# Three 256-column products into the same 256 columns, in place of a 512-column product, a 256-column one and a fold

## What is computed

```python
def glu_out(y, h):                      # end of the S5 mixer
    z = jax.nn.gelu(y...); a, g = jnp.split(z @ w_glu, 2, axis=-1)
    return a * jax.nn.sigmoid(g)

def sq_relu_mlp(h, w1, w2):             # w1: 2048 x 8192, w2: 8192 x 2048
    return jnp.square(jax.nn.relu(h @ w1)) @ w2

def swiglu(h, w_gate, w_up, w_down):    # D_FF = 5632
    return (jax.nn.silu(h @ w_gate) * (h @ w_up)) @ w_down

# first_block
x_lat = x_lat + gt1[:, None] * rmsnorm(y_lat, norm_mix_post[layer])
h_lat = modulate(rmsnorm(x_lat, norm_mlp_pre[layer]), sh2[:, None], sc2[:, None])
x_lat = x_lat + gt2[:, None] * rmsnorm(sq_relu_mlp(h_lat, ...), norm_mlp_post[layer])

# second_block
for layer in range(2):
    h = rms_norm(x, mix_norm_g[layer])
    if layer == 0:
        z = h @ ab_w_in[0]              # 2048 x 4096: a, gate, u, v, 1024 each
        y_conv = conv_module(z[..., :2048], ...)      # a * sigmoid(gate), 31 taps in time, layer norm, silu
        y_sgu = spatial_gating(z[..., 2048:], ...)    # gelu, layer norm of v, mixed over tokens, times u
        x = x + jnp.concatenate([y_conv, y_sgu], axis=-1) @ ab_w_out[0]
    else:
        x = x + fourier_mix(h) @ fnet_w_out[0] + fnet_b_out[0]
    h = rms_norm(x, ffn_norm_g[layer])
    x = x + swiglu(h, w_gate[layer], w_up[layer], w_down[layer])
return rms_norm(x, final_norm_g)
```

## Time and profile before

| | us |
|---|---|
| time, median of 3 (lowest, highest) | 3479.0 (3478.8, 3480.57) |
| time of the profiled execution | 3470.21 |
| span in its profile | 3468.3 |
| TensorE busy | 3227.5 (93%) |
| VectorE busy | 2201.4 (63%) |
| ScalarE busy | 1389.7 (40%) |
| GpSimd busy | 480.2 (14%) |
| granted clock of TensorE, mean | 0.96 |
| weights and all else read | 637.28 MB, 185 GB/s over the span |

### The profile page before, as it was taken

How to read it: one execution, slowest core, us unless ns; L and a number is a source line. 1 busy time by engine, 2 the same in 40 slices (tenths; PEclk the granted TensorE clock), 3 DMA queues, 4 the chain that set the end, 5 groups by cost and what they waited for, 6 DMA issues and landing times.

```text
span 3468.3 us, 51580 instructions
## 1 busy us (share of the span) xinstructions
PE 3227.5 (93%) x21009; PEld 2726.8 (79%) x21009; DVE 2201.4 (63%) x1891; ACT 1389.7 (40%) x1433; POOL 480.2 (14%) x352
## 2 busy tenths in 40 slices
PE   5788899799999999798599999999999999999998
PEld 3445578588888888676488888888878888888887
DVE  7668754555655555679757656665674765566565
ACT  4446643433333333332234434433333443443332
POOL 2979700000000000069000000000000000000000
PEclk7889999899999999998799999999999999999999
DMA  9998975355555555344145555555544555555552
GB/s 297 300 301 255 272 243 183 101 170 193 176 196 185 190 185 189 102 157 151 49 146 184 192 185 181 184 201 182 194 152 134 183 183 196 178 194 194 189 186 85
DMA packets 351027, 643.17 MB, mean 185 GB/s; under 512 B 21599, under 2 KB 50359, under 8 KB 350519
## 3 DMA queue, kind: packets, MB, share of 16 engines
q1 hardware_dynamic: 309952, 561.42, 49.7%
q10 hardware_dynamic: 40951, 79.98, 6.8%
HBM read 637.28 MB, written 4.06 MB: 185 GB/s over the span
## 4 chain that ended last, share of the span: by engine, by line
PE 82%; DVE 6%; DMA 3%; issue 3%; POOL 2%; ACT 2%; SPq 1%; DVEq 1%; ACTq 0%; POOLq 0%
PE acc L455 50%; PE acc L456 26%; DMA raw<-in_w_mod_dram 2%; PE acc L1274 1%; DVE z L1060 1%; DVE w_lo L849 1%; POOL cpow L1927 1%; PE acc L1366 1%; POOL ptmp L1927 1%; ACT u L1528 1%; PE acc L1349 1%; DMA tw<-r_scratch 1%; PE acc L475 0%; DMA r_scratch<-rw 0%; PE acc L553 0%
## 5 line engine op out<-in xcount | busy, mean ns | idle before, releaser
L849 DVE TENSOR_TENSOR w_lo<-raw,w_hi 128x2048 fp32r<-128x2048 f32 x484 | 1109.3, 2300 | 962.9 <-ACT w_hi L672 961.4
L455 PE MATMUL acc<-xin,w_hi 128*128 128x512 f32 x3968 | 1417.4, 400 | 44.0 <-DVE w_lo L849 24.1
L672 ACT ACTIVATE w_hi<-raw 128x2048 fp32r<-128x2048 f32 x484 | 924.7, 1917 | 1231.9 <-PE acc L456 1231.8
L455 PE MATMUL acc<-hid,w_hi 128*128 128x512 f32 x3840 | 1332.7, 391 | 0.0
L456 PE MATMUL acc<-xin,w_lo 128*128 128x256 f32 x3968 | 1122.5, 283 | 0.0
L456 PE MATMUL acc<-hid,w_lo 128*128 128x256 f32 x3840 | 1075.3, 280 | 0.0
L455 PEld LDWEIGHTS acc<-xin,w_hi 128*128 128x128 f32 x3968 | 752.1, 190 | 232.6 <-DVE w_lo L849 25.4
L455 PEld LDWEIGHTS acc<-hid,w_hi 128*128 128x128 f32 x3840 | 718.2, 187 | 157.9
L456 PEld LDWEIGHTS acc<-xin,w_lo 128*128 128x128 f32 x3968 | 755.4, 190 | 0.0
L456 PEld LDWEIGHTS acc<-hid,w_lo 128*128 128x128 f32 x3840 | 725.8, 189 | 0.1
L855 DVE TENSOR_REDUCE tmp<-acc 128x1024 f32<-128x2048 f32 x116 | 264.9, 2283 | 21.9 <-PE acc L456 21.9
(11 more groups left out here) (265 smaller groups left out, 2088.5 us busy)
## 6 DMA issues: line engine op xcount, KB each, us to landing
raw<-in_ffn_w_gate_dram SPq DMA_DIRECT2D x88, 1024.0 KB, 5.2
raw<-in_ffn_w_up_dram SPq DMA_DIRECT2D x88, 1024.0 KB, 5.2
raw<-in_ffn_w_down_dram SPq DMA_DIRECT2D x88, 1024.0 KB, 5.1
raw<-in_w_mod_dram ACTq DMA_DIRECT2D x76, 1024.0 KB, 8.9
raw<-in_w_mlp_in_dram SPq DMA_DIRECT2D x64, 1024.0 KB, 5.2
raw<-in_w_mlp_out_dram SPq DMA_DIRECT2D x64, 1024.0 KB, 5.1
raw<-in_s_w_glu_dram SPq DMA_DIRECT2D x32, 1024.0 KB, 5.4
raw<-in_ab_w_in_dram SPq DMA_DIRECT2D x32, 1024.0 KB, 5.3
```

What stands on the lines that cost most here:

```text
L455: pe.matmul(bank, w_hi[:, slot, w], operand[:, kt, :], start=(kt == 0), stop=False)
L672: act.activation(w_hi[:, slot, :], raw[:, slot, :, :].rearrange("p k n -> p (k n)"), ACT.Copy).then_inc(hi_ready, 1)
L849: dve.tensor_tensor(w_lo[:, slot, :], raw[:, slot, :, :].rearrange("p k n -> p (k n)"), w_hi[:, slot, :].bitcast(F32), SUB).then_inc(lo_re ...
```

## The change

In `block_` the tile becomes three matmuls of 256 columns: `w_hi` times the high columns, `w_hi` times the low columns and `w_lo` times the high columns, all accumulated in columns 0 to 255 of the bank. These columns of four banks have a name now, `sums[half]`, and nothing is left to fold. `fold` is a plain copy and stands in three places (the GLU's first half and two blocks of AB_IN); elsewhere the consumer reads the banks: ScalarE's sigmoid, gelu and a new relu, VectorE's products, and `fold_into`, which adds the sums to `y` or `xr`. The FFN adds its down blocks to `xr` directly, so the additions to `y`, the zeroing of `y` and the additions of `y` to `xr` are gone. In `gate_up` the second product with rstd is gone: rstd is multiplied to the gate twice, before and after silu. `folded` counts the release of the banks by whichever engine reads them, and takes over from several semaphores. ScalarE's reads of banks stand in its own program before the split that they once followed.

```diff
+        sums = [acc[:, 4 * h:4 * h + 4, 0:TOK] for h in range(2)]
...
@@ SyncE
-            sp.wait_ge(x_new, 4 * NCK)
+            sp.wait_ge(x_rs, 3)
             sp.dma_start(dft[:, :], a["c_dft"]).then_inc(dft_in, 16)
...
@@ TensorE, block_
-                            bank, kt = ps[4 * half + n], UK * k + q
-                            pe.matmul(bank, w_hi[:, slot, w], operand[:, kt, :], start=(kt == 0), stop=False)
-                            ins = pe.matmul(bank[:, 0:TOK], w_lo[:, slot, w], operand[:, kt, 0:TOK],
-                                            start=False, stop=(kt == UK * units - 1))
+                            o, kt = ps[4 * half + n][:, 0:TOK], UK * k + q
+                            pe.matmul(o, w_hi[:, slot, w], operand[:, kt, 0:TOK], start=(kt == 0), stop=False)
+                            pe.matmul(o, w_hi[:, slot, w], operand[:, kt, TOK:2 * TOK], start=False, stop=False)
+                            ins = pe.matmul(o, w_lo[:, slot, w], operand[:, kt, 0:TOK], start=False, stop=(kt == UK * units - 1))
...
@@ ScalarE, GLU
-                    split(g, slots=(2, 3))
-                act.wait_ge(folded, 2 * i + 2)
-                act.activation(tmp[:, 1], tmp[:, 1], ACT.Sigmoid).then_inc(gate_act, 1)
+                    split(g, slots=(2,))
+                    if g == 2 * i + 2:
+                        act.wait_ge(pe_unit, 4 * g)
+                        act.wait_ge(folded, 2 * i + 1)
+                        act.wait_ge(y_added, i + 1)
+                        act.activation(tmp[:, 1], sums[1], ACT.Sigmoid).then_inc(folded, 1)
+                    split(g, slots=(3,))
...
@@ ScalarE, MLP
                         split(8 * q + (2 * i + (G + 1 + j)))
-                        hidden(4 * q + (2 * i + j), 2 * i + j, j, hid)
+                        act.wait_ge(pe_unit, 32 * q + (8 * i + (MLP[0] + 4 * j + 4)))
+                        act.wait_ge(hid_ready, 4 * q + (2 * i + (j + 1)))
+                        act.activation(tmp[:, j], sums[j], ACT.Relu).then_inc(relu_done, 1)
+                        hidden(8 * q + (2 * i + (MLP[1] + j)), 2 * i + j, j, hid)
...
@@ ScalarE, AB_IN
+            for j in range(8):
+                split(G + 1 + j)
+                if j in (0, 2):
+                    continue
+                place, func = {1: (8, ACT.Sigmoid), 3: (12, ACT.Sigmoid)}.get(j, (4 * j, ACT.Gelu))
+                act.wait_ge(pe_unit, AB_IN[0] + 4 * j + 4)
+                act.wait_ge(folded, AB_IN[1] + j)
+                act.activation(z[:, place:place + 4, :], sums[j % 2], func).then_inc(folded, 1)
...
@@ VectorE
-            def fold(units_done, half, dst, done=None):
+            def fold(units_done, half, dst):
 
                 dve.wait_ge(pe_unit, units_done)
-                dve.tensor_reduce(dst, acc[:, 4 * half:4 * half + 4, :].rearrange("p a (t b) -> p a b t", t=2),
-                                  AX.X, ADD).then_inc(folded, 1)
+                dve.tensor_copy(dst, sums[half]).then_inc(folded, 1)
+
+            def fold_into(units_done, blk, half, dst):
+
+                dve.wait_ge(pe_unit, units_done)
+                dve.wait_ge(folded, blk)
+                dve.tensor_tensor(dst, dst, sums[half], ADD).then_inc(folded, 1)
...
@@ VectorE, gate_up of the FFN
                     split(grp + 1)
-                    dve.wait_ge(y_added, added)
                     dve.wait_ge(hid_ready, n + 1)
-                    fold(4 * grp + 4, 0, tmp[:, 0])
-                    dve.wait_ge(folded, blk + 1)
+                    dve.wait_ge(pe_unit, 4 * grp + 4)
+                    dve.wait_ge(folded, blk)
+                    dve.tensor_tensor(tmp[:, 0], sums[0], rstd, MUL).then_inc(folded, 1)
+                    split(grp + 2, (0,))
+                    dve.wait_ge(gate_act, gate + 1)
                     dve.tensor_tensor(tmp[:, 0], tmp[:, 0], rstd, MUL).then_inc(scaled, 1)
-                    split(grp + 2)
-                    fold(4 * grp + 8, 1, tmp[:, 1])
-                    dve.wait_ge(folded, blk + 2)
-                    dve.tensor_tensor(tmp[:, 1], tmp[:, 1], rstd, MUL).then_inc(scaled, 1)
-                    dve.wait_ge(gate_act, gate + 1)
-                    dve.wait_ge(scaled, nth + 2)
-                    dve.tensor_tensor(tmp[:, 1], tmp[:, 1], tmp[:, 0], MUL).then_inc(h_ready, 1)
+                    split(grp + 2, (1, 2, 3))
+                    dve.wait_ge(pe_unit, 4 * grp + 8)
+                    dve.wait_ge(scaled, gate + 1)
+                    dve.tensor_tensor(tmp[:, 1], sums[1], tmp[:, 0], MUL).then_inc(folded, 1)
                     hidden(n, c, 1, xin)
...
@@ VectorE, last part of the FFN
-                    add_to_y(4 * g2 + REST * (c + 1), b2 + c, c % 2, c, y1 + c, h1 + REST + 1)
-                    dve.wait_ge(y_added, y1 + c + 1)
-                    dve.tensor_tensor(xr[:, chunk(c), :], xr[:, chunk(c), :], y[:, chunk(c), :], ADD).then_inc(x_new, 1)
+                    fold_into(4 * g2 + REST * (c + 1), b2 + c, c % 2, xr[:, chunk(c), :])
...
@@ VectorE, AB_IN
             for j in range(8):
-                place = (0, 8, 4, 12, 16, 20, 24, 28)[j]
                 split(G + 1 + j)
-                fold(AB_IN[0] + 4 * j + 4, j % 2, z[:, place:place + 4, :])
+                if j in (0, 2):
+                    dve.wait_ge(folded, AB_IN[1] + j)
+                    fold(AB_IN[0] + 4 * j + 4, 0, z[:, 4 * (j // 2):4 * (j // 2) + 4, :])
...
@@ GpSimd
-            for n in (2, 4):
-                pool.wait_ge(x_rs, n + 1)
-                pool.memset(yflat, 0.0).then_inc(y_zero, 1)
```

More of the change, by code:

```diff
@@ L683, in seam @@
                     for c in range(NCK):
-                        act.wait_ge(y_added, (Y_MLP, Y_FFN0)[s.n] - NCK + c + 1)
+                        act.wait_ge(*((y_added, c + 2) if s.n == 0 else (folded, s.block - NCK + c + 1)))
                         act.activation(s.sq[:, CH * c:CH * (c + 1), :], y[:, CH * c:CH * (c + 1), :], ACT.Square).then_inc(y_sq, 1)
@@ L713, in join_raw, with hidden @@
                 act.activation(rs[:, 1, :], rs[:, 1, :], ACT.Sqrt).then_inc(x_root, 1)
-            def hidden(n, chunk, half, dst):
-                act.wait_ge(h_ready, n + 1)
+            def hidden(blk, chunk, half, dst):
+                act.wait_ge(folded, blk + 1)
                 act.activation(dst[:, ds(CH * chunk, CH) if not isinstance(chunk, int) else slice(CH * chunk, CH * (chunk + 1)), 0:TOK],
@@ L779, in GEMM_ACT @@
             G = AB_IN[0] // 4
-            for half in range(2):
-                split(G + 1 + 2 * half)
-                split(G + 2 + 2 * half)
-                act.wait_ge(folded, AB_IN[1] + 2 * half + 2)
-                gate = z[:, 8 + 4 * half:12 + 4 * half, :]
-                act.activation(gate, gate, ACT.Sigmoid).then_inc(gate_sig, 1)
-            with act.Fori(0, 2) as i:
-                split(i + (G + 5))
-            act.wait_ge(folded, AB_IN[1] + 6)
-            act.activation(z[:, 16:24, :], z[:, 16:24, :], ACT.Gelu).then_inc(u_gelu, 1)
-            with act.Fori(0, 2) as i:
-                split(i + (G + 7))
-            act.wait_ge(folded, AB_IN[1] + 8)
-            act.activation(z[:, 24:32, :], z[:, 24:32, :], ACT.Gelu).then_inc(v_gelu, 1)
+            for j in range(8):
[6 more added lines that the diff above has]
+                act.activation(z[:, place:place + 4, :], sums[j % 2], func).then_inc(folded, 1)
             act.wait_ge(ws_tr, 1)
@@ L1019, in GEMM_DVE @@
                 split(2 * i + 2)
-                fold(8 * i + 8, 1, tmp[:, 1])
-                dve.wait_ge(gate_act, i + 1)
+                dve.wait_ge(folded, 2 * i + 2)
                 dve.tensor_tensor(y[:, chunk(i), :], tmp[:, 0], tmp[:, 1], MUL).then_inc(y_added, 1)
@@ L1031, in GEMM_DVE @@
                         split(8 * q + (2 * i + (G + 1 + j)))
-                        dve.wait_ge(y_added, 4 * q + Y_MLP)
-                        dve.wait_ge(hid_ready, n + 1)
-                        fold(32 * q + (8 * i + (MLP[0] + 4 * j + 4)), j, tmp[:, j])
-                        dve.wait_ge(folded, 8 * q + (2 * i + (MLP[1] + j + 1)))
-                        dve.scalar_tensor_tensor(tmp[:, j], tmp[:, j], 0.0, tmp[:, j], ALU.max, MUL).then_inc(h_ready, 1)
+                        dve.wait_ge(relu_done, n + 1)
+                        dve.wait_ge(folded, 8 * q + (2 * i + (MLP[1] + j)))
+                        dve.scalar_tensor_tensor(tmp[:, j], sums[j], 0.0, tmp[:, j], ALU.max, MUL).then_inc(folded, 1)
                         hidden(n, 2 * i + j, j, hid)
```

91 lines of the change are left out of this document (38 added, 53 removed).

## The result

The changed kernel takes 3515.65 us (median of 4 runs, 3510.41 to 3519.56) against 3478.9 before: a ratio of 1.011, 95% interval 1.0094 to 1.0125. It is slower by 37 us. The forecast was 3483, at most 3506.

The account below looks back on a forecast made before the run. TensorE was taken as the bound, nearly all in the weight products' matmuls. +13.1 (hid) +10.6 (xin) -19.9 (removals) gave +3.8 us: 3474.0 for the profiled execution, 3483 for the median, range 3457 to 3506.

Parts of the forecast that it names:

- so the load stays hidden, with only 7 ns in hand: Weight-product tiles: a third weight load, at 109 ns, fits beside a 256-column matmul of 116.7 ns.
- if each takes what the short one takes now: Tiles with hid: three 256-column matmuls take 350.1 ns, 3.4 ns more a tile, +13.1 us over 3840 tiles.
- the weight load comes through: First rival, chance 0.14: the load shows at each tile's middle matmul; 3505 with xin alone, 3552 if everywhere.
- Its far form: First rival with 120.8 ns for every matmul: +60 us with hid, +33 with xin, less 19.9: +73, 3552.
- the bound: Tiles with xin: +2.9 ns a tile, +10.6 us, bounded by 350.1 (-12 us) and 362.4 ns (+33 us).
- GLU: End of the GLU: sigmoid reads the bank ahead of ScalarE's split, squares begin earlier, -4.5 us, between -3.4 and -6.
- inner waits: Last gate and up step of each FFN: the chain to TensorE's hidden values loses a fold and a product, -1.6 us.
- the ends of the FFNs: TensorE's two waits for the last square go, since fold and second addition go: -1.8 us.
- AB_IN: VectorE-bound convolution stage: five folds go, 11.0 us, and one becomes a copy, 1.0 us: -12.0 us.
- Code loading: Fourth rival, chance 0.12: the MLP's longer loop body makes three jumps back wait for instructions, +6 us, 3489.
- The free split: Second rival, chance 0.15: halves of the 512-column matmul take 115 ns each, hid and xin pay nothing, 3459.
- The alternation: Third rival, chance 0.11: xin's slow and fast tiles come from the 512-column read and vanish, 3460, or 3471 if half goes.

Follow-up runs that it names:

- experiment 3: The kernel before with hid and all buffers behind it moved by 32 bytes: 3472.5 us, ratio 0.9982.
- experiment 2: The changed kernel with hid and all buffers behind it moved by 32 bytes: 3476.05 us, ratio 1.0001.
- experiment 4: The changed kernel with each tile's second and third matmul exchanged: 3511.9 us, ratio 1.0101.
- experiment 1: The kernel before with only the 512-column matmul split into two of 256 columns, into separate bank columns: 3530.5 us, ratio 1.0155.

## Why the prediction was wrong

**The step that failed** is "so the load stays hidden, with only 7 ns in hand", and with it "if each takes what the short one takes now". The 7 ns came from transposes, 109 ns apart, whose stream is 128 columns; beside a stream of 256 columns each load takes 113 to 120 by placement, and in hid's placement 120.0. In the tile before, two loads of 113 are 227 of 347 ns, so there is room to cover what placement adds (experiment 3: the parts move, the sum doesn't); three of them fill the new tile. The experiments show that third load and the placement are the cost; that one load was covered by the 512 columns is argued from the sums. The term of +13.1 us for hid measured +50.4. The forecast tile of 350 did appear once hid lay 32 bytes further (experiment 2), but by another cause than the one that the prediction gave, which knew nothing of placement. The rival "the weight load comes through" was the right mechanism in the main, with 0.14 of the chance, and with its place wrong: not the repeated w_hi load (experiment 4), and not xin, which I thought the weaker, but hid. Its far form, with 120.8 for every matmul, was near the 120.0 that hid took, and I left it outside the range. I counted "hid tiles show no waiting at all" against it; that was no evidence, since a tile with room for its loads shows none.

**xin.** +1.7 ns a tile in place of +2.9, so +6.3 us for +10.6; the bound held. The even share of slow and fast did not stay: about three in 8 matmuls are slow.

**Folds and waits.** GLU, inner waits and the ends of the FFNs came as worked out. AB_IN gave 9.3 in place of 12.0 us. The steps of the convolution got longer, here those of the kernel before and of the changed one, in the stretch in which GpSimd works beside VectorE and in the stretch after it:

```profile
L1060 DVE SCALAR_TENSOR_TENSOR z<-conv_in,par,z 128x256 f32<-128x256 f32 x180 | 101.1, 635 | 0.0
```

```profile
1530.00:1650.00 120.00, 69.34 (x112) 0.89 0.42 144
1655.00:1680.00 25.00, 14.06 (x37) 0.65 0.48 168
```

```profile
L1044 DVE SCALAR_TENSOR_TENSOR z<-conv_in,par,z 128x256 f32<-128x256 f32 x180 | 104.1, 652 | 0.0
```

The first and last rows are groups of the page, the kernel before first; the two between are windows of the kernel before. Beside GpSimd the busy time for each record is 69.34/112 = 619 ns, alone 14.06/37 = 380 (records overlap; by their starts steps alone follow each other after 396 ns). GpSimd's share takes nearly as long as before, 128.5 us from VectorE's first step of the convolution where it was 130.4, so in a stage cut by 11 us more steps run beside it: 137 of 180, where it was 127, and 127 too in experiment 1, which keeps the folds. 17 ns x 180 = 3.1 us, about the missing part. This is read from the traces; no run tested it.

**Code loading** did not come: 24 packets more, 1.26 times and not 1.5, and no gap. **The free split** fell with experiment 1. **The alternation** with xin changed its form and hardly its mean.

The sum by the measured terms: 50.4 + 6.3 - 4.8 - 9.3 - 1.6 - 2.8 = +38 against a forecast of +3.8.

## What to carry to other kernels

Before splitting a wide matmul, count weight loads against streamed columns: where each load has only 256 columns to hide beside, the load is the bound, and the row of a kernel in which it was covered doesn't show its price. To see it, look for matmuls with a full load and few columns (113 ns here) and compare the starts, not the busy share of PEld: that follows from the starts. In a kernel that is bound by loads, try the addresses: 32 bytes between operand and weights were 40 us of 3500 here, and the placement has to be measured, since it can't be worked out from the distance alone. Compare two designs each in a good placement: as they stood, the change lost 37 us, and with the same shifts it won 50. Against the kernel before in the best of its four placements (3472.5) it is 47.

## What the runs showed of the hardware

- Matmuls of 256 columns with a load of a 128x128 fp32r tile each stand 113.3 to 120.0 ns apart by placement at granted clock 1.00 (113.3, 116.7, 117.8, 118.3 and 120.0 were seen). Three loads with 512 columns among them take 340 ns at 1.00 and 640 at 0.50, so 113.3 and 213 each. With 32 columns to stream, a load of 128 columns takes 113 too.
- With half of the columns of two of three matmuls left out, the granted clock was 0.50 in most of the stretch from the start of the MLP to the first FFN, though the profile shows TensorE busy all the time in the MLP: 4252 us, in one run. With one of three it stayed at 1.00 in the MLP.
- Two programs that were profiled twice kept their pitches, stage by stage, to 0.02 us in a block sequence without waits.
- On VectorE, steps of the convolution (128x256) follow each other after 396 ns alone; with GpSimd at work beside it the busy time for each is 619 ns in place of 380.
